# Attention of a hybrid encoder layer: softmax division moved behind the value product, splits moved to GpSimd

## The reference, cut to what matters

```python
s = jnp.einsum('bqkgd,bskd->bkgqs', qblk, k).astype(jnp.float32) * scale
p = jax.nn.softmax(s, axis=-1).astype(v.dtype)
return jnp.einsum('bkgqs,bskd->bqkgd', p, v)
...
mixed = jnp.concatenate([attn_out, lru_out], axis=-1)
x = x + jnp.einsum('bse,ed->bsd', mixed, w_out)
```

## Time and profile before

| what | value |
|---|---|
| median of 3 runs | 1011.89 us (1011.80 to 1012.08) |
| profiled execution, its own time | 1012.73 us |
| its span, first to last instruction | 1010.7 us |
| PE, DVE, ACT, POOL busy | 97%, 82%, 72%, 17% of the span |
| slots: first scores, last value product | 203.05 us, 327.80 us |
| output projection of block 1 starts | 334.09 us |

### The profile page before, as it was taken

One profiled execution on the slowest core, in us unless ns is written; L12 is line 12 of the kernel. 1 busy time (PEld: TensorE's weight loads), 2 busy tenths in 40 slices (PEclk: granted clock), 3 DMA queues, 4 the chain that ended last, 5 costly groups with the idle time before them and its releaser, 6 DMA issues.

```text
span 1010.7 us, 15239 instructions
## 1 busy us (share of the span) xinstructions
PE 981.9 (97%) x5076; PEld 826.8 (82%) x5076; DVE 830.2 (82%) x1063; ACT 732.6 (72%) x982; POOL 173.2 (17%) x195
## 2 busy tenths in 40 slices
PE   8999999999999999969999999999999999999997
PEld 8997998877878788857888888888888888888885
DVE  6659898989885543667989998999999899989995
ACT  7447897487994334447878887888888788878873
POOL 1000000043793321250100110110011001101001
PEclk9999999999999999979999999999999999999999
DMA  7110111001102635379999999999999999999972
GB/s 269 49 43 21 37 38 43 1 1 64 63 2 66 213 121 177 118 267 398 409 391 392 390 412 392 392 393 409 392 392 405 397 392 391 410 392 392 390 273 62
DMA packets 75315, 248.98 MB, mean 246 GB/s; under 512 B 9421, under 2 KB 16649, under 8 KB 75273
## 3 DMA queue, kind: packets, MB, share of 16 engines
q1 hardware_dynamic: 70472, 231.12, 59.0%
q0 software_dynamic: 4784, 17.30, 6.5%
q10 hardware_dynamic: 16, 0.00, 0.0%
HBM read 231.63 MB, written 16.78 MB: 246 GB/s over the span
## 4 chain that ended last, share of the span: by engine, by line
PE 87%; DVE 5%; ACT 3%; DMA 2%; issue 2%; POOL 1%; POOLq 0%; ACTq 0%; DVEq 0%
PE bank L1097 25%; PE bank L1099 25%; PE bank L1098 25%; PE bank L1103 6%; DMA raw_gate<-in_exp_w_gate_dram 2%; PE bank L1263 1%; PE bank L1262 1%; PE bank L1295 1%; POOL prob L667 1%; DVE e_lo L1905 1%; PE bank L1147 1%; PE bank L1402 1%; POOL wo_lo L659 0%; DVE row_stat L1713 0%; ACT e_hi L1025 0%
## 5 line engine op out<-in xcount | busy, mean ns | idle before, releaser
L1097 PE MATMUL bank<-e_hi,xsT_hi 128*128 128x512 f32 x508 | 199.7, 393 | 1.3 <-DVE e_lo L1905 1.3
L1099 PE MATMUL bank<-e_hi,xsT_lo 128*128 128x512 f32 x508 | 197.8, 389 | 0.0
L1098 PE MATMUL bank<-e_lo,xsT_hi 128*128 128x512 f32 x508 | 197.8, 389 | 0.0
L1025 ACT ACTIVATE e_hi<-raw_gate 128x1024 fp32r<-128x1024 f32 x128 | 134.8, 1061 | 35.0 <-PE bank L1099 29.3
L1905 DVE TENSOR_TENSOR e_lo<-raw_gate,e_hi 128x1024 fp32r<-128x1024 f32 x126 | 149.5, 1221 | 6.1 <-ACT e_hi L1025 2.3
L1905 DVE TENSOR_TENSOR e_lo<-raw_down,e_hi 128x1024 fp32r<-128x1024 f32 x128 | 149.5, 1220 | 4.4 <-ACT e_hi L1025 1.4
L1905 DVE TENSOR_TENSOR e_lo<-raw_up,e_hi 128x1024 fp32r<-128x1024 f32 x128 | 148.4, 1220 | 4.5 <-ACT e_hi L1025 3.2
L1025 ACT ACTIVATE e_hi<-raw_down 128x1024 fp32r<-128x1024 f32 x128 | 128.4, 1060 | 11.8 <-PE bank L1099 11.8
L1025 ACT ACTIVATE e_hi<-raw_up 128x1024 fp32r<-128x1024 f32 x128 | 126.8, 1057 | 2.7 <-PE bank L1099 1.2
L1097 PEld LDWEIGHTS bank<-e_hi,xsT_hi 128*128 128x128 f32 x508 | 95.4, 188 | 22.1 <-DVE e_lo L1905 3.0
L1099 PEld LDWEIGHTS bank<-e_hi,xsT_lo 128*128 128x128 f32 x508 | 95.4, 188 | 19.9
(11 more groups left out here) (305 smaller groups left out, 2022.2 us busy)
## 6 DMA issues: line engine op xcount, KB each, us to landing
raw_gate<-in_exp_w_gate_dram SPq DMA_DIRECT2D x64, 1024.0 KB, 18.2
raw_up<-in_exp_w_up_dram SPq DMA_DIRECT2D x64, 1024.0 KB, 18.8
raw_down<-in_exp_w_down_dram SPq DMA_DIRECT2D x64, 1024.0 KB, 18.5
w_raw<-in_w_in_dram SPq DMA_DIRECT2D x6, 1024.0 KB, 5.4
wo_raw<-in_w_out_dram SPq DMA_DIRECT2D x8, 512.0 KB, 4.3
y_dram<-x SPq DMA_DIRECT2D x8, 512.0 KB, 5.2
h_rows<-h SPq DMA_DIRECT2D x8, 512.0 KB, 2.7
x_nat<-in_x_prompt_dram SPq DMA_DIRECT2D x4, 512.0 KB, 6.0
```

The costliest lines, as they stand in the source:

```text
L1025: act.activation(e_hi[:, (8 * m + j) % SPLIT, :], raw[:, j // 2, j % 2, :], ACT.Copy).then_inc(row_hi, inc)
L1097: pe.matmul(out, l_hi, r_hi, start=first, stop=False)
L1098: pe.matmul(out, l_hi, r_lo, start=False, stop=False)
L1099: return pe.matmul(out, l_lo, r_hi, start=False, stop=last)
```

## The change

The exponentials are turned as they are (`exp_done` in place of `prob_done`). POOL's multiplication of each unit is gone. Values are held as high, low, high again (`v_parts`; POOL copies the second high part), so that one 128-column weight block holds both parts of one head. A block of values is now two matmuls, by the turned high and the turned low part; one half of the 128 output rows is the product with the high values, the other with the low ones. Each head has its own bank use: ACT copies the low-value rows (`low_half`), DVE the high-value rows (`high_half`), one slot after the head's last product; for even heads from head 2 on both wait first for the `mixA_lo_done` of the pair before. DVE takes the reciprocals of eight units at once, POOL spreads them over 64 columns each (`spread_recip`, slots 11, 19, ... 67), PE turns them (`spread_shares`, slots 15, 23, ... 71) and ACT copies them out (`shares`, one slot later). POOL's `finish_pair` (slots 18, 26, 34, ... 74) adds the halves, multiplies, makes mixA_hi and mixA_lo. V_LAG becomes 9. With bank 7 taken by turns and shares, heads 0 to 6 share bank 6. POOL's splits at the slots listed above now make the high half too, with a wait on its own semaphore between the two; ACT's 20 are gone. The zero fills of v are gone. Some single semaphores of DVE outside attention are replaced by a common counter, with the same waits.

```diff
-    VW = (2 * KVH + 1) * HD
-    v_hi = [at(f"v_hi{s}", R1 + o * K, [P, BPS, VW], F32R) for s, o in enumerate((80, 90))]
-    v_lo = [at(f"v_lo{s}", R1 + o * K, [P, BPS, VW], F32R) for s, o in enumerate((97, 85))]
+    v_parts = [at(f"v_parts{s}", R1 + (80 + 6 * s) * K, [P, BPS, KVH, 3, HD], F32R) for s in range(SEQS)]
+    low_half = at("low_half", R1 + 92 * K, [P, S], F32)
+    high_half = at("high_half", R1 + 94 * K, [P, S], F32)
+    shares = at("shares", R1 + 96 * K, [P, S], F32)
+    spread = at("spread", R1 + 98 * K, [P, BPS, 2, HD], F32)
...
-    T_LAG, V_LAG = 6, 8
+    T_LAG, V_LAG = 6, 9
...
+    HEADS_ONE_BANK = 7
+    SHARES_AT = {8 * pair + 6 + V_LAG: pair for pair in range(HEADS // 2)}
...
-    PAIRS_ONE_BANK = 3
-    def out_bank(pair):
-        return 6 if pair < PAIRS_ONE_BANK or pair % 2 == 0 else 7
-    def late_pair(v):
-        return v % (2 * BPS) == 0 and 0 < v // (2 * BPS) < PAIRS_ONE_BANK
+    def out_bank(head):
+        return 6 if head < HEADS_ONE_BANK or head % 2 == 0 else 7
+    def shares_bank(pair):
+        return 7 if 2 * pair + 1 < HEADS_ONE_BANK else 6
+    def late_head(v):
+        return v % BPS == 0 and 0 < v // BPS < HEADS_ONE_BANK
...
+    def ended_head(u):
+        v = u - V_LAG - 1
+        return v // BPS if 0 <= v < UNITS and v % BPS == BPS - 1 else None
+    def value_rows(head):
+        return slice(head % 2 * HD, head % 2 * HD + HD)
...
-        for s in range(SEQS):
-            pool.wait_ge(proj_done, NG * JOBS if s else (NG - 1) * JOBS)
-            for v in (v_hi[s], v_lo[s]):
-                pool.memset(v[:, :, :].bitcast(F32).rearrange("p b (g d) -> p b g d", d=HD)[:, :, 0::2, :], 0.0).then_inc(v_zeroed, 1)
+        own = [0]
+        def link(ins):
+            own[0] += 1
+            ins.then_inc(pool_step, 1)
+            pool.wait_ge(pool_step, own[0])
+        def copy_v(s):
+            pool.wait_ge(v_hi_done, s + 1)
+            pool.tensor_copy(v_parts[s][:, :, :, 2, :], v_parts[s][:, :, :, 0, :]).then_inc(v_copied, 1)
+        def spread_recip(pair):
+            pool.wait_ge(recip_done, pair + 1)
+            if pair:
+                pool.wait_ge(shares_turned, pair)
+            shares_of = row_stat[:, 2, 2 * BPS * pair:2 * BPS * (pair + 1)].rearrange("p (h q) -> p q h", h=2)
+            pool.tensor_copy(spread[:, :, :, :], shares_of.unsqueeze(3).to_broadcast([P, BPS, 2, HD])).then_inc(spread_done, 1)
+        def finish_pair(pair):
+            pool.wait_ge(low_done, 2 * pair + 2)
+            pool.wait_ge(high_done, 2 * pair + 2)
+            link(pool.tensor_tensor(high_half[:, :], high_half[:, :], low_half[:, :], ALU.add))
+            pool.wait_ge(shares_copied, pair + 1)
+            link(pool.tensor_tensor(high_half[:, :], high_half[:, :], shares[:, :], ALU.mult))
+            link(pool.tensor_copy(mixA_hi[mix_of(pair)], high_half[:, :]))
+            pool.tensor_tensor(mixA_lo[mix_of(pair)], high_half[:, :], mixA_hi[mix_of(pair)].bitcast(F32), ALU.subtract).then_inc(mixA_lo_done, 1)
+        copy_v(0)
         for kind, n in attn:
-            if kind == "split_lo" and n < 2 * WO_EARLY:
+            if kind == "v":
+                copy_v(n)
+            elif kind == "split_lo" and n < 2 * WO_EARLY:
                 k, cols = n // 2, slice(n % 2 * D // 2, (n % 2 + 1) * D // 2)
-                pool.wait_ge(wo_hi_done, n + 1)
+                pool.wait_ge(wo_loaded[k], 16)
+                link(pool.tensor_copy(wo_hi[k][:, cols], wo_raw[k][:, cols]))
                 pool.tensor_tensor(wo_lo[k][:, cols], wo_raw[k][:, cols], wo_hi[k][:, cols].bitcast(F32), ALU.subtract).then_inc(wo_lo_pool, 1)
             elif kind == "split_lo":
                 i, cols = (n - 2 * WO_EARLY) // 2, slice(n % 2 * S, (n % 2 + 1) * S)
-                pool.wait_ge(mixL_hi_done, n - 2 * WO_EARLY + 1)
+                pool.wait_ge(scores_done, BPS * HQ)
+                pool.wait_ge(gated, SEQS * CT)
+                link(pool.tensor_copy(mixL_hi[:, i, cols], lru_out[:, i, cols]))
                 pool.tensor_tensor(mixL_lo[:, i, cols], lru_out[:, i, cols], mixL_hi[:, i, cols].bitcast(F32), ALU.subtract).then_inc(mixL_lo_done, 1)
-            elif kind == "slot" and 0 <= n - 1 < UNITS:
-                u = n - 1
-                pool.wait_ge(recip_done, u + 1)
-                pool.tensor_scalar(prob[:, u % PROB_SLOTS, :], prob[:, u % PROB_SLOTS, :], row_stat[:, 2, u:u + 1], 1.0,
-                                   ALU.mult, ALU.mult).then_inc(prob_done, 1)
+            elif kind == "slot" and ended_head(n - 1) is not None and ended_head(n - 1) % 2:
+                finish_pair(ended_head(n - 1) // 2)
+            elif kind == "slot" and n + 4 in SHARES_AT:
+                spread_recip(SHARES_AT[n + 4])
...
-            elif kind == "split_hi":
-                if n < 2 * WO_EARLY:
-                    split_wo_hi(n // 2, n % 2)
-                else:
-                    i, cols = (n - 2 * WO_EARLY) // 2, slice(n % 2 * S, (n % 2 + 1) * S)
-                    act.wait_ge(scores_done, BPS * HQ)
-                    act.wait_ge(gated, SEQS * CT)
-                    act.activation(mixL_hi[:, i, cols], lru_out[:, i, cols], ACT.Copy).then_inc(mixL_hi_done, 1)
             elif kind == "slot":
-                u, t, v = n, n - T_LAG, n - V_LAG - 1
-                if v >= 0 and v % (2 * BPS) == 2 * BPS - 1:
-                    pair = v // (2 * BPS)
...
-                    act.wait_ge(pv_done, v + 1)
-                    act.activation(mixA_hi[:, head % HQ // 2, head // HQ * S:(head // HQ + 1) * S], bank[:, out_bank(pair), :],
-                                   ACT.Copy).then_inc(mixA_hi_done, 1)
+                u, t, head, pair = n, n - T_LAG, ended_head(n), SHARES_AT.get(n - 1)
+                if head is not None:
+                    act.wait_ge(pv_done, BPS * (head + 1))
+                    if head % 2 == 0 and head:
+                        act.wait_ge(mixA_lo_done, head // 2)
+                    act.activation(low_half[value_rows(head), :], bank[value_rows(head + 1), out_bank(head), :], ACT.Copy).then_inc(low_done, 1)
+                if pair is not None:
+                    act.wait_ge(shares_turned, pair + 1)
+                    if pair:
+                        act.wait_ge(mixA_lo_done, pair)
+                    act.activation(shares[:, :], bank[:, shares_bank(pair), :], ACT.Copy).then_inc(shares_copied, 1)
...
+        act.wait_ge(mixA_lo_done, HEADS // 2)
...
-            pair, s = head // 2, head // HQ
-            if kc == 0 and head % 2 == 0 and pair:
-                pe.wait_ge(mixA_lo_done, pair if pair < PAIRS_ONE_BANK else pair - 1)
-            pe.wait_ge(v_lo_done, s + 1)
-            pe.wait_ge(v_zeroed, 2 * (s + 1))
+            s, g, odd = head // HQ, head % HQ // (HQ // KVH), head % 2
+            if kc == 0 and head:
+                gone = head if head < HEADS_ONE_BANK else head - 1
+                pe.wait_ge(low_done, gone)
+                pe.wait_ge(high_done, gone)
+                if head == HEADS_ONE_BANK:
+                    pe.wait_ge(*turn_out(USES * NB - 2))
+                    pe.wait_ge(*turn_out(USES * NB - 1))
+                if head >= HEADS_ONE_BANK:
+                    pe.wait_ge(shares_copied, head // 2)
+            if kc == 0:
+                pe.wait_ge(v_lo_done, s + 1)
+                pe.wait_ge(v_copied, s + 1)
             pe.wait_ge(probT_lo_done, v + 1)
-            cols = pair_cols(head)
-            product(bank[:, out_bank(pair), :], v_hi[s][:, kc, cols], v_lo[s][:, kc, cols], probT_hi[:, kc, :], probT_lo[:, kc, :],
-                    head % 2 == 0 and kc == 0, head % 2 == 1 and kc == BPS - 1).then_inc(pv_done, 1)
+            both_parts = v_parts[s][:, kc, g, odd:odd + 2, :].rearrange("p a d -> p (a d)")
+            out = bank[:, out_bank(head), :]
+            pe.matmul(out, both_parts, probT_hi[:, kc, :], start=(kc == 0), stop=False)
+            pe.matmul(out, both_parts, probT_lo[:, kc, :], start=False, stop=(kc == BPS - 1)).then_inc(pv_done, 1)
+        def spread_shares(pair):
+            pe.wait_ge(spread_done, pair + 1)
+            if shares_bank(pair) == 7:
+                before = [n for n in range(EARLY, USES * NB) if slot_of_turn(n) < 8 * pair + 6 + V_LAG]
+                pe.wait_ge(*turn_out(before[-1]))
+                pe.wait_ge(*turn_out(before[-2]))
+            else:
+                pe.wait_ge(low_done, 2 * pair + 1)
+                pe.wait_ge(high_done, 2 * pair + 1)
+            transposes(shares_bank(pair), [spread[:, qb, :, :].rearrange("p h d -> p (h d)") for qb in range(BPS)], shares_turned)
...
-                    pe.wait_ge(prob_done, BPS * (head + 1))
+                    pe.wait_ge(exp_done, BPS * (head + 1))
...
+                if u in SHARES_AT:
+                    spread_shares(SHARES_AT[u])
...
-                u, t, v = n, n - T_LAG, n - V_LAG - 1
+                u, t, head = n, n - T_LAG, ended_head(n)
                 if u < UNITS:
```

(22 more changed lines are left out.)

49 lines of the change are left out of this document (21 added, 28 removed).

## The result

| | before | after |
|---|---|---|
| median of 4 runs each | 1011.99 us | 1027.78 us (1025.50 to 1028.21) |
| ratio, 95% interval | | 1.0151 [1.0136, 1.0165] |
| profiled execution; span | 1012.73; 1010.7 | 1028.14; 1026.3 |

1.5% slower. The direction was forecast, the size was not: +15.8 us where +8 was forecast, and 1027.78 lies above the range (1013 to 1026).

What follows compares the result with a forecast made beforehand. PE was taken to bound the attention slots before, POOL slots 34 to 58 afterwards. Slots 7 to 32 -4.5, slot 33 to the last value product +9.2, tail +3.5: +8.2 on 1011.89, said 1020.0 us; range 1013.0 to 1026.0.

Steps and rivals of the forecast that it cites:

- POOL's queue: Slots 34 to 58: 17 splits, three spreads, three `finish_pair` take POOL 50.8 us against PE's 34.1; loss 9.2 us.
- the price of a copy: POOL's one-input 128x512 copy in each split: taken as 0.69 us, with 0.60 and 0.90 as ends.
- PE's three waits: Slots 34 to 58: three idle times of PE of 3 to 8 us, ended by ACT or DVE.
- its one-input rule: POOL's copies at roughly line-rate: 0.60 us each, POOL's sum 1.8 us less; set aside for the multiplication's 0.693.
- the tail: Last value product to block 1: `finish_pair(7)` and DVE's four low halves take turns, 3.5 us more; bounds -0.3 and 3.5.
- a mere shift: Behind block 1: all waits are relative, so the whole shifts and no time is gained or lost there.
- slots 7 to 32: First attention stretch: 44.9 us instead of 49.39, a gain of 4.5 us.
- Floors of the three engines afterwards: Slots 7 to 32: least time by engine, PE 41.7, DVE 41.2, ACT 39.7 us.
- I allow 3.2 us: Slots 7 to 32: allowance over the highest floor for close engines and head changes in one bank, giving 44.9 us.
- The clock rival: Between `finish_pair` calls: POOL bound, and PE's clock falls after idling; 1023 to 1027 us, chance 0.14.
- six at 1.5 us eat the 4.5: Rival, slots 13 to 33: head changes in one bank bind and cancel the gain; 1024.5 us, part of the range.
- a gain of 0 to 7: Slots 7 to 32: bounds on the gain in us, 0 if every head change costs 1.5 us.

Runs made afterwards that it cites:

- e8: Changed kernel, with POOL's last `finish_pair` held until DVE's four low halves of w_out are done and PE awaiting the last mixA only where used: 1025.56 us.
- e9: Changed kernel, with the low parts of q and k (blocks 5 to 7) and of the second v moved from DVE to POOL: 1022.59 us, 1.0100.
- e10: Changed kernel, with the 20 splits spread over slots 25 to 70 and the tail order of e8: 1014.52 us, 1.0023.
- e12: Kernel of e11 with the low parts of q, k and v on POOL as in e9: 1008.67 us, 0.9964.
- e11: Kernel of e10 with heads alternating between banks 6 and 5 and two turn banks: 1012.62 us, 1.0005.
- e13: Kernel before the change, with only the edit of e9 (low parts of q, k and v on POOL): 1010.31 us, 0.9978.

## Why the prediction was right and wrong

**Right: the direction and what decides it.** POOL's queue bounds slots 34 to 58. The forecast 50.8 us from `finish_pair(2)` to `finish_pair(5)` was 48.2 (271.48 to 319.67), and POOL waited for nobody in it. Most of the rest is the price of a copy: I took 0.69 us from a multiplication, and it was 0.61. The nearest row was the wrong neighbour. PE's three waits were 2.69, 3.78 and 2.86 us (forecast 3 to 8), and the first and the last were ended by POOL's spread, not by ACT or DVE. The Trainium skill, "GPSIMD Engine Reference", section "4. When to use GPSIMD", was nearer: by its one-input rule I had worked out 0.60 and 1.8 us less for this sum. The cast's 0.61 us agrees with it. I had the rule beside me and gave it too little weight.

**Right, with some luck: the tail.** +3.5 was forecast from two instructions of the earlier trace rows taken by turns, +3.9 came. k = 6 started 4.57 us behind the last value product (forecast 4.85). e8 shows the cause by taking it away. The Trainium skill, "SBUF — State Buffer", section "SBUF: two separate sides", calls it an exclusive lock, and the 5.75 us against 2.50 agree in the main (the last section has the rest). Two errors cancelled: DVE's last low half ended 7.2 us behind the last value product and not 8.1, and the clock, which I had not priced, took that back. The twelve matmuls of k = 6 and 7 took 5.43 us (344.56 to 349.99) where before they took 2.90, at 0.43 us each, the 1.2 GHz level, instead of 0.23. At the older pace block 1 would have started some 8.7 us behind the last value product (7.2 and half of 2.90, my estimate), +2.6 and not +3.9.

**Right: behind block 1 a mere shift.** Block 1 starts 15.90 us later, the span is 15.6 longer. PE's idle 6.01 us of the earlier trace rows is there unchanged:

```profile
457.26 0.61 PE L1433 MATMUL bank<-small,minus_by_group 128*128 128x18 f32 x2 [6.01 <-POOL minus_by_group L754]
```

**Wrong: slots 7 to 32, by 8.3 us.** The step was "Floors of the three engines afterwards", 41.7, 41.2 and 39.7 us, and over them "I allow 3.2 us". The floors were near enough: a slot without extras takes the forecast 1.37 us behind slot 34, and PE's floor is if anything 1 us too high, since slots 7 and 8 have no value product. The 3.2 us were 11.5. Three things are wrong with the step.

First and largest, the allowance treated three floors within 5% of each other as if they ran side by side. Row maximum (DVE), exponential (ACT), high part (ACT) and low part (DVE) pass each slot to and fro between the two, and DVE's extra work adds to that circle: taking 3.3 us of it away gave 3.7 (e9 against e10) and 3.6 (e12 against e11), all at a clock of 1.00. Nor did PE alone bound the stretch before, as the prediction says: the same edit took 2.8 us off it (e13), most of the 3.8 by which it exceeded PE's floor of 45.6. That the saved matmuls uncovered more of these waits fits the 3.7 us against 2.8, but is argued. The groups of before point to the circle in a row that I did not use: over the 64 slots DVE stood 18.6 us before its low parts, 18.1 of it for ACT.

```profile
L1725 DVE TENSOR_TENSOR probT_lo<-bank,probT_hi 128x512 fp32r<-128x512 f32 x64 | 43.7, 685 | 18.6 <-ACT probT_hi L946 18.1
```

Second, the clock in this stretch, which the step put at nothing: 1.6 us (after against e10). It fell behind PE's longest wait, 2.21 us at a change of heads. The clock rival (1023 to 1027) came nearest in number, but its place was the slots behind 33, and they were 0.8 us shorter than forecast: there the half-clock stretches were hidden by POOL.

Third, the changes of heads in one bank. I had this as a rival ("six at 1.5 us eat the 4.5") and held it for part of the range. Its sign came: PE waited 7.0 us at five changes, up to 2.2 at one, because the copy that frees the bank stands in the most loaded queue. Its price did not: with a second bank the stretch is 1.0 us shorter at equal clock, as DVE and ACT are behind with or without these waits. What they cost beyond that is the lower clock that can follow them.

**The range.** It failed at its upper end because the bounds of that stretch were a gain of 0 to 7. A loss was not among them, though nothing excluded one.

**What stays open.** Of the 8.3 us, 1.6 are the clock, 3.6 DVE's extra work and 1.0 the bank. The lowest value with both edits, 47.0 (e12), is still 2.1 above the forecast 44.9. Its trace shows two waits of PE of that size together, in slots 15 and 23, where it turns the shares:

```profile
226.67 0.61 ACT L866 ACTIVATE qT<-bank 128x512 fp32r<-128x512 f32 x1
...
227.37 0.63 PE L1159 MATMUL bank<-ident,spread 128*128 128x128 f32 x4 [1.07 <-issue]
...
241.92 0.59 ACT L866 ACTIVATE qT<-bank 128x512 fp32r<-128x512 f32 x1
...
242.90 0.63 PE L1159 MATMUL bank<-ident,spread 128*128 128x128 f32 x4 [1.05 <-ACT qT L866]
```

Shares and turned heads use bank 7 by turns, and the shares wait until ACT has copied a turned head out of it. Neither moving that copy nor taking other work off ACT, busy 42.88 us there, was tried.

## What to carry to other kernels

When the bounding engine gets work taken off and two others stand within a tenth of it, add up what those two hand to each other per round before you book the gain; equal busy times with none full were the mark of such a circle here. A copy that frees a buffer is late by what stands ahead of it in its engine's queue. But a wait that shows in the profile is not its price: moving this copy forward gave 1.1 us and a second bank 1.0, where PE's waits added up to 7.0; taking 3.3 us of work off the queue gave 3.7. And compare stretches at equal granted clock: a fall of the clock behind a long wait was worth 1.6 us here, more than the second bank. Work that is moved to an idle engine must be spread over that engine's idle time: the same 20 splits took 11.0 us more packed into 28 slots than spread over 45.
